# Gate columns of a hybrid layer's input projection: from weights stationary to activations stationary, with the heads' steps moved

## The reference

```python
h = rmsnorm(x, g_mix_pre);  proj = h @ w_in
mq, mk, mv, mo, mi, mf, rq, rk, rv, rg = split(proj)
mq, mk = silu(causal_dwconv([mq, mk]))
hm = head_rmsnorm(mlstm_chunkwise(mq, mk, mv, mi, mf), g) * sigmoid(mo)
hr = head_rmsnorm(retention_chunkwise(rotary(rq), rotary(rk), rv), g) * silu(rg)
x = x + rmsnorm(concat(hm, hr) @ w_out, g_mix_post)
h = rmsnorm(x, g_ffn_pre)
x = x + rmsnorm((silu(h @ w_gate) * (h @ w_up)) @ w_down, g_ffn_post)
```

## Time and profile before

| | us |
|---|---|
| median of 3 runs (1235.53 to 1236.18) | 1235.66 |
| the profiled execution: its time | 1235.49 |
| its span, first to last instruction | 1233.5 |
| busy: TensorE matmul / weight load | 1219.8 / 1026.0 |
| busy: VectorE / ScalarE / GpSimd | 704.3 / 598.9 / 12.4 |

### The profile page before, as it was taken

One profiled execution on the slowest core, in us unless ns is written; L12 is line 12 of the kernel. 1 busy time (PEld: TensorE's weight loads), 2 busy tenths in 40 slices (PEclk: granted clock), 3 DMA queues, 4 the chain that ended last, 5 costly groups with the idle time before them and its releaser, 6 DMA issues.

```text
span 1233.5 us, 15772 instructions
## 1 busy us (share of the span) xinstructions
PE 1219.8 (99%) x5907; PEld 1026.0 (83%) x5907; DVE 704.3 (57%) x898; ACT 598.9 (49%) x781; POOL 12.4 (1%) x35
## 2 busy tenths in 40 slices
PE   8999999999999999999999999999999999999997
PEld 7888888888888888888888888888888888888886
DVE  6656767777676646754554455454455454444444
ACT  5454666574655644644444444444444444343442
POOL 1000100000000000000000000000000000000000
PEclk9999999999999999999999999999999999999999
DMA  8566798967887566455565656565555665555551
GB/s 313 188 157 159 148 214 173 142 181 164 204 178 177 205 204 206 140 200 188 187 189 186 196 178 203 177 197 189 185 188 186 203 208 203 193 184 203 192 183 69
DMA packets 136936, 229.48 MB, mean 186 GB/s; under 512 B 6080, under 2 KB 55488, under 8 KB 136384
## 3 DMA queue, kind: packets, MB, share of 16 engines
q1 hardware_dynamic: 136608, 226.84, 62.9%
q0 software_dynamic: 288, 2.10, 0.5%
HBM read 226.83 MB, written 2.10 MB: 186 GB/s over the span
## 4 chain that ended last, share of the span: by engine, by line
PE 92%; DMA 4%; DVE 2%; ACT 1%; issue 0%; DVEq 0%; SPq 0%; ACTq 0%
PE bank L1142 91%; DMA raw<-in_w_in 3%; PE bank L1386 1%; DVE w_lo L726 1%; ACT w_hi L428 1%; DMA resid<-in_x 0%; DVE h L757 0%; PE bank L1304 0%; PE bank L1147 0%; DVE resid L1014 0%; ACT h L459 0%; PE bank L1359 0%; DVE gT L894 0%; ACT L555 0%; DVE pre L861 0%
## 5 line engine op out<-in xcount | busy, mean ns | idle before, releaser
L726 DVE TENSOR_TENSOR w_lo<-raw,w_hi 128x1024 fp32r<-128x1024 f32 x420 | 513.4, 1225 | 492.3 <-ACT w_hi L428 492.1
L428 ACT ACTIVATE w_hi<-raw 128x1024 fp32r<-128x1024 f32 x420 | 444.0, 1060 | 574.3 <-PE bank L1142 554.9
L1142 PE MATMUL bank<-w_hi,h2T 128*128 128x512 f32 x1376 | 426.6, 390 | 0.0
L1142 PEld LDWEIGHTS bank<-w_hi,h2T 128*128 128x128 f32 x1376 | 258.3, 188 | 53.4
L1142 PE MATMUL bank<-hT,w_hi 128*128 128x512 f32 x768 | 271.3, 397 | 0.0
L1142 PE MATMUL bank<-w_lo,h2T 128*128 128x512 f32 x688 | 267.7, 389 | 0.0
L1142 PE MATMUL bank<-w_hi,ffT 128*128 128x512 f32 x704 | 217.0, 389 | 0.0
L1142 PE MATMUL bank<-hT,w_lo 128*128 128x256 f32 x768 | 214.4, 279 | 0.0
L1142 PEld LDWEIGHTS bank<-hT,w_hi 128*128 128x128 f32 x768 | 144.0, 188 | 32.4
L1142 PEld LDWEIGHTS bank<-w_hi,ffT 128*128 128x128 f32 x704 | 132.2, 188 | 27.4
L1142 PEld LDWEIGHTS bank<-w_lo,h2T 128*128 128x128 f32 x688 | 129.2, 188 | 26.4
(11 more groups left out here) (159 smaller groups left out, 549.0 us busy)
## 6 DMA issues: line engine op xcount, KB each, us to landing
raw<-in_w_in SPq DMA_DIRECT2D x63, 1024.0 KB, 12.5
raw<-in_w_gate SPq DMA_DIRECT2D x44, 1024.0 KB, 5.2
raw<-in_w_up SPq DMA_DIRECT2D x44, 1024.0 KB, 5.1
raw<-in_w_down SPq DMA_DIRECT2D x44, 1024.0 KB, 5.0
raw<-in_w_out SPq DMA_DIRECT2D x16, 1024.0 KB, 5.1
resid<-in_x SPq DMA_DIRECT2D x2, 1024.0 KB, 5.9
out<-resid SPq DMA_DIRECT2D x8, 256.0 KB, 2.5
raw<-in_w_in SPq DMA_DIRECT2D x2, 512.0 KB, 8.5
```

The source lines that it names most:

```text
L428: act.activation(w_hi[:, s % AHEAD, :], raw[:, s // 2, (s % 2) * SUB:(s % 2 + 1) * SUB], ACT.Copy).then_inc(hi_done, 1)
L726: dve.tensor_tensor(w_lo[:, s % AHEAD, :], raw[:, s // 2, (s % 2) * SUB:(s % 2 + 1) * SUB], w_hi[:, s % AHEAD, :].bitcast(F32), ALU.subtra ...
L1142: return pe.matmul(out_, lhsT, rhs, start=start, stop=stop, skip_group_check=True)
```

## The change

The gate rounds use `sub_tokens` instead of `sub_columns`: one accumulator pair for a whole round, tokens on partitions. Their weights are loaded as 4 rows x 512 columns per partition instead of 8 x 256. ScalarE takes the sigmoid (or, for retention, silu) straight from the accumulators into `gate_out` at s = 7, `head_scaled` multiplies `y` by it, and `mix`, the gate sums, the gate's `copy_right` and the later multiplication by the pre-activation disappear. `mix_hi` and `mix_rest` now both read bank `B_T`. With the gate known only at the round's end, every head step starts four subs later (`HEAD_LAG`); `mix_hi` moves from 7 to 6 and `mix_rest` from 8 to 7 after the start, and `turned` (now `head_turned`) waits for `mix_lo`. Output groups 0 and 1 are interleaved: six subs of 0, six of 1, two of 0, two of 1, then group 2. TensorE's loop over groups becomes straight code.

```diff
+HEAD_LAG = 4
+OUT_SUBS = [(0, k) for k in range(6)] + [(1, k) for k in range(6)] + [(0, 6), (0, 7), (1, 6), (1, 7)]\
+    + [(2, k) for k in range(8)]
+OUT_ENDS = {13: 0, 15: 1, 23: 2}
...
-        n, odd = divmod(8 * (rnd - gate_round(group)) + s - first, 2)
+        n, odd = divmod(8 * (rnd - gate_round(group)) + s - HEAD_LAG - first, 2)
...
+                            if n == 2:
+                                src = in_rows(4 * q, 4, col, 512)
+                            else:
+                                src = in_rows(8 * (q % 2), 8, col + (q // 2) * 256, 256)
...
-                a = head_at(rnd, s, 7)
+                a = head_at(rnd, s, 6)
                 if a is not None:
-                    act.wait_ge(mix_ready, a + 1)
-                    act.activation(mixT[:, a, 0:SEQ], gT[:, a % 4, :], ACT.Copy).then_inc(mix_hi, 1)
+                    act.wait_ge(yT_done, a + 1)
+                    act.activation(mixT[:, a, 0:SEQ], bank[:, B_T, 0:SEQ], ACT.Copy,
+                                   scale=coef[:, C_GHEAD + a:C_GHEAD + a + 1]).then_inc(mix_hi, 1)
...
+                if is_gate(rnd) and s == 7:
+                    event = event_of(rnd, 0)
+                    act.wait_ge(acc_free, event + 2)
+                    for t in range(TT):
+                        ins = act.activation(gate_out[:, t, :], acc(pair_used(event))[:, t, :],
+                                             ACT.Silu if rnd >= gate_round(2) else ACT.Sigmoid)
+                    ins.then_inc(acc_free, 1)
...
+                dve.wait_ge(acc_free, event_of(gate_round(a // 4), 0) + 3)
                 for t in range(TT):
-                    ins = dve.tensor_scalar(y[:, a % 2, t, :], pv_out(a)[:, t, 0:HD],
-                                            head_stat(a, H_SCALE)[:, t:t + 1], None, ALU.mult)
+                    ins = dve.scalar_tensor_tensor(y[:, a % 2, t, :], pv_out(a)[:, t, 0:HD],
+                                                   head_stat(a, H_SCALE)[:, t:t + 1],
+                                                   gate_out[:, t, a % 4 * HD:(a % 4 + 1) * HD],
+                                                   ALU.mult, ALU.mult)
                 ins.then_inc(y_ready, 1)
-
-            def mix(a):
...
             def mix_rest(a):
                 dve.wait_ge(mix_hi, a + 1)
-                dve.tensor_tensor(mixT[:, a, SEQ:2 * SEQ], gT[:, a % 4, :],
-                                  mixT[:, a, 0:SEQ].bitcast(F32), ALU.subtract).then_inc(mix_lo, 1)
+                dve.scalar_tensor_tensor(mixT[:, a, SEQ:2 * SEQ], bank[:, B_T, 0:SEQ],
+                                         coef[:, C_GHEAD + a:C_GHEAD + a + 1],
+                                         mixT[:, a, 0:SEQ].bitcast(F32),
+                                         ALU.mult, ALU.subtract).then_inc(mix_lo, 1)
...
-                for step, first in ((weigh, 0), (mix, 6), (head_scaled, 4), (head_variance, 3),
-                                    (head_recip, 2), (mix_rest, 8)):
+                for step, first in ((weigh, 0), (head_scaled, 4), (head_variance, 3), (head_recip, 2),
+                                    (mix_rest, 7)):
...
+            def head_turned(a):
+                pe.wait_ge(y_ready, a + 3)
+                if a:
+                    pe.wait_ge(mix_lo, a)
                 for t in range(TT):
-                    ins = pe.transpose(bank[:, B_T, t * P:(t + 1) * P], y[:, n % 2, t, :], ident)
+                    ins = pe.transpose(bank[:, B_T, t * P:(t + 1) * P], y[:, a % 2, t, :], ident)
                 ins.then_inc(yT_done, 1)
...
+                if is_gate(rnd):
+                    event = event_of(rnd, 0)
+                    pe.wait_ge(acc_free, event + 1)
+                    for s in range(8):
+                        heads_in_front(rnd, s)
+                        sub_tokens(8 * rnd + s + 1, s % AHEAD, hT, pair_used(event), 2 * s, KT - 1)
+                        heads_behind(rnd, s)
```

More of the change, by code:

```diff
@@ L353, in _ @@
                         for q in range(4):
[L354 to L359, removed]
+                            col = COL_RET * kind + 512 * half + part * DH
+                            if n == 2:
+                                src = in_rows(4 * q, 4, col, 512)
+                            else:
+                                src = in_rows(8 * (q % 2), 8, col + (q // 2) * 256, 256)
+                            load(6 * kind + 3 * half + (R_IN + n), q, src)
+            for m in range(16):
+                g, k = OUT_SUBS[2 * m] if m < 12 else (3, 2 * (m - 12))
+                load(R_OUT + m // 4, m % 4, rows(w_out, 2 * k, 4, 512 * g, 512))
             with sp.Fori(0, FF_GROUPS) as i:
@@ L548, in mixer_step @@
                 if ended:
[L549 to L556, removed]
+                    event = event_of(rnd, ended[2])
+                    copy_right(pair_used(event), event)
+                if is_gate(rnd) and s == 7:
[5 more added lines that the diff above has]
+                    ins.then_inc(acc_free, 1)
                 ended = unit_at(rnd, s, 2)
-                if ended and ended[1] < 2:
+                if ended:
                     group, part, u = ended
@@ L1164, in sub_columns, with unit_columns @@
                 ins.then_inc(sub_done, 1)
[L1166 removed]
+            def unit_columns(rnd, unit, act_T, before, after):
+                event = event_of(rnd, unit)
                 pe.wait_ge(acc_free, event + 1)
@@ L1305, in turned @@
                 ins.then_inc(yT_done, 1)
-            def gate_units(group, rnd, event):
-                def before(s):
-                    if s % 2 == 0:
-                        scores(group, s // 2)
-                def after(s):
-                    if s % 2 == 1:
-                        weighted(group, s // 2)
-                        if s >= 5:
-                            turned(group, (s - 5) // 2)
-                for u in range(2):
-                    unit_columns(rnd, u, event + u, hT, before, after)
@@ L1344, in _, with heads_in_front @@
[L1344 to L1351 removed]
+            def heads_in_front(rnd, s):
+                a = head_at(rnd, s, 0)
+                if a is not None:
+                    scores(a)
@@ new lines, in heads_behind @@
+            def heads_behind(rnd, s):
+                for step, first in ((weighted, 1), (head_turned, 5)):
+                    a = head_at(rnd, s, first)
+                    if a is not None:
+                        step(a)
+                if (rnd, s) == (R_IN, 3):
+                    pe.wait_ge(gates_act, 1)
+                    pe.wait_ge(gates_dve, 2)
+                if (rnd, s) == (R_IN, 6):
+                    gate_columns()
+                if rnd == R_IN + 1 and s == 0:
+                    spread_rows()
```

143 lines of the change are left out of this document (59 added, 84 removed).

## The result

The changed kernel takes **1254.25 us** (median of 4 runs, 1252.89 to 1256.39) beside 1235.92 us of the kernel before on the same chip: ratio 1.0143, 95% interval 1.0129 to 1.0158. That is 18 us slower, four times the 4.3 us that were forecast, and outside the range. The profiled execution took 1252.89 us with a span of 1251.2 us, 17.7 us more than the 1233.5 us of before.

A forecast was written before the change was run, and what follows sets the result against it. TensorE's matmuls, 91% of the chain, were taken as the bound. Gains of 4.1 us against waits of 7.8 and 0.9 gave +4.6 us, about 1240.0 us for the median, 0.35% slower; range 1232.5 to 1242.5 us.

The forecast's parts named there:

- the line on loads: Gate weights arrive in 2 KB runs, not 1 KB; ScalarE sometimes waits for such loads, TensorE does not: costed at nothing.
- the one on straight code: TensorE runs at full pace both in the loop and outside it, so writing the loop out was costed at nothing.
- The wait that the change adds: TensorE's transposes wait until `mix_rest` frees bank `B_T`: 7.8 us behind sub 13 plus 0.9 behind sub 15.
- behind sub 13: Sixth sub of the next q round, counting from the gate round's start: waits of 2.7, 2.3, 2.3 and 0.5 us.
- Behind sub 15: Last sub of the next q round: `w_lo`, then `mix_rest`; 0.2 us in three groups, 0.36 in the output projection, sum 0.9.
- the bold rule: An unobstructed VectorE head step ends about one sub late, just when TensorE comes to its own step of the same number.
- Rivals A and B: A: waits absent or small, 1231.6 to 1233.8 us, 17%. B: half the waits, 1235.9 us, 18% with what falls short of 2.5.
- The gain of 4.1 us: TensorE's total saving: 1.6 us from the gate rounds' form, 2.2 from the excess, 0.3 from a wait in the output projection.
- The term of 2.2 us for the excess: Extra 1.35 and 0.87 us in the 13-sub stretches of groups 0 and 2 should go through the head steps' four-sub lag.
- its 0.4 us per gate round: Gate subs by tokens take 2.72 us instead of 2.77: 0.05 us each, 1.6 us over 32 subs.
- Rival C: Matmul pace set half by weight load, half by columns: token form gains 11 us, 1229 even with all waits; 3%.
- Rival D: The gate activation's cover is gone too, at `head_scaled`: up to 1 us more in four groups, 1244 us; 12%.

The follow-up runs named there:

- e1: The kernel before with only TensorE's loop over the three groups written out as straight code; 1252.10 us, ratio 1.0116.
- e3: The changed kernel with q, k and gate weights all loaded as 4 rows of 512 columns (2 KB runs); 1243.44 us, ratio 1.0051.
- e15: The kernel of e2 with one more input of 1.5 MB that no instruction reads; 1235.90 us, ratio 0.9992.
- e2: The changed kernel with `mix_rest` issued a step earlier and first in VectorE's turn; 1249.73 us, ratio 1.0098.
- e10: The kernel of e2 with all these weight loads in 2 KB runs, as in e3; 1233.91 us, ratio 0.9987.
- e9: The kernel before with all loads of the projection's 12 rounds in 2 KB runs; 1235.01 us, ratio 0.9992.
- e13: The kernel before with one more input of 1 MB that no instruction reads; 1238.54 us, ratio 1.0029.
- e5: The kernel before with TensorE's loop over the feed-forward groups written out, nothing changed in the mixer; 1258.50 us, ratio 1.0182.
- e8: The kernel of e2 with one more input of 1 MB that no instruction reads; 1248.64 us.

## Why the prediction was wrong, by its steps

- **The step that failed is the line on loads, "ScalarE waits for such loads at times, TensorE does not, so no gain", with the one on straight code, "both at full pace": both were costed at nothing.** The heading promised their cover, and for the loads none was worked out. Loads landed up to 23.3 us after their issue in the kernel before, ScalarE waited for them 19.4 us in all, and at about 25 us TensorE waits on `w_lo`: a cover of 2 us at best. In one place there was none. The load of 23.3 us, issued at 134 us, landed at 157.4; ScalarE had waited for it, VectorE came late to `probs`, and TensorE waited for that, in the kernel before:

```profile
157.60 2.01 ACT L428 ACTIVATE w_hi<-raw 128x1024 fp32r<-128x1024 f32 x2 [2.23 <-DMA raw<-in_w_in]
```

```profile
163.83 0.93 PE L1142 MATMUL bank<-v_sb,probs 128*128 x6 [0.91 <-DVE probs L912]
```

  The edit that writes TensorE's code out was priced by its pace alone. In this kernel it changes how long loads take, and costs 1252.10 - 1236.85 = 15.3 us by itself in e1 (its own runs of before beside it). In the changed kernel the late loads are 1254.25 - 1243.44 = 10.8 us (e3; 11.7 us against each one's runs of before), or 13.8 us once the other wait is out of the way (e15 against e2).
- **The wait that the change adds was right in place, order and nearly in size.** The prediction had 2.7, 2.3, 2.3 and 0.5 us behind sub 13. Behind the q round of group 1, TensorE's last matmul starts at 210.27 and is done 0.11 later (half of one pace), the transpose starts at 213.13: 2.75 us. The other gaps are 2.35, 2.34 and some 0.4. VectorE's rows there are the ones that were counted, rotation or convolution first, `mix_rest` (line 973) after it, and the restart 0.15 us behind its end at 212.98:

```profile
211.64 0.87 DVE L910 SCALAR_TENSOR_TENSOR pre<-pre,columns,spin 128x256 f32<-128x256 f32 x2
212.43 0.16 DVE L953 TENSOR_SCALAR stat<-stat 128x2 f32<-128x2 f32 x1
212.50 0.48 DVE L973 SCALAR_TENSOR_TENSOR mixT<-bank,columns,mixT 128x256 fp32r<-128x256 f32 x1
```

  Behind sub 15 the gaps are 0.3, 0.2, 0.2 and 0.3 us, 1.1 in place of 0.9, so all gaps are 8.9 us where the term was 8.7. The 9.4 us between the spans of e3 and e10 hold these 8.9 us, 1.7 us of lower clock behind the first gap of e3 ((0.39 + 0.18) x 3, from 204 to 210 us; in the changed kernel the clock stayed at 1.00 behind the same gap) and 0.4 us of pace (below), less 1.7 us of gaps that e10 has itself: 9.3 us. Taking `mix_rest` one step earlier removes the wait, as the bold rule says, at the price of one of these: 1.3 us once in front of a transpose that waits for `y`, since VectorE now waits 1.9 us for ScalarE's half of `mixT`. Rivals A and B are out.
- **The gain of 4.1 us was too high.** The 13-sub stretches hold 41.79, 41.65 and 42.39 us (the differences in the table's rows) in place of 43.15, 41.80 and 42.67, 1.8 us less in three groups. In e3 against e9 the change costs 8.4 us with a wait of 9.5: a net gain of 1.1 us at most. The term of 2.2 us for the excess had a wrong cause: in e9, where only the loads differ from before and the heads' steps stand as they did, the stretches are 41.8, 42.0 and 41.9 us, and in e13 group 1 has the long one (43.7 us) and not group 0. The excess was late loads too, as the rows at 157.60 and 163.83 above show for group 0. And the form did not give its 0.4 us per gate round: from the start of group 1's gate round to the end of the q round behind it the kernel before takes 50.1 us and e10 50.7, where 49.7 was forecast. Of this 1.0 us the pace, the point below, is 0.4, and a gap of 0.2 is left in front of the transpose behind sub 13; the rest was not settled.
- **"Both at full pace" for straight code was wrong by a small amount.** Column subs run at two paces. e10, TensorE at the first matmul of two subs in an early round, and at the same matmul (the eighth) of two subs in a late one:

```profile
145.06 0.40 PE L1157 MATMUL bank<-hT,w_hi 128*128 128x512 f32 x1
...
147.88 0.40 PE L1157 MATMUL bank<-hT,w_hi 128*128 128x512 f32 x1
...
358.93 0.28 PE L1157 MATMUL bank<-hT,w_lo 128*128 128x256 f32 x1
...
361.70 0.28 PE L1157 MATMUL bank<-hT,w_lo 128*128 128x256 f32 x1
```

  2.82 us against 2.77. Counted over the sub starts of the trace, 5 column subs went at 2.82 to 2.83 us in the kernel before and 10 in e9, but 20 in e10 and 27 in e3: 17 more between e9 and e3 at 0.055 us, 0.9 us. What sets the pace was not settled: e13, the kernel before with an unread input, has 25.
- **Rival C is out**: the gate rounds by tokens gave no 11 us, not even without waits (e10), nor the 8 us that I had estimated beside it from the Trainium skill (TensorE: Matmul & The Clock Gate, Back-to-back issue gap); by that page's paces the measurement disagrees, with 227 ns for a matmul of 512 columns. **Rival D is out too**: the waits of the changed kernel have no line for a late gate activation of the size it needed, and the emptying of output group 0 stayed covered.
- The chance of "slower" (0.62) was right in sign, but the range had no case in which the loads become the bound. The prediction's range went to 1242.5; e3, where only the known terms act, is at 1243.44, 6.6 us over its own runs of before, which is 1242.3 from the prediction's 1235.66: just inside. (By the prediction's own list "same" is 0.18 and "faster" 0.20, where it says 0.19 for both.)

What stays open is the property of the memory behind it. These runs show that the length of a program and an unread input move it, that it goes where all these loads have 2 KB runs (which also read the rows in another order, so that the run length alone is not isolated), and that in e2's kernel 64 KB, 512 KB and 2 MB do nothing, 1 MB swaps the halves, and 1.5 MB brings back the landings of the kernel before. How the length of a program does it is open too: e5 brought 0.66 MB of instructions where before brings 0.43 MB, a smaller difference than the 512 KB that did nothing. The Trainium skill (DMA: Bandwidth & Descriptors, Latency and other measured facts) tells of copies that slow down when the rows of neighbouring partitions lie large powers of two apart, and gives aliasing of memory channels as an inference. `w_in` has 16 rows of 8208 floats for each partition, 513 KB apart, near such a distance; but the same row of the page has hardly any loss at 512 KB (207 GB/s, beside 214 for a padded one), for 16 KB per partition, where 1 KB runs moved 120 GB/s here. No run here varied the distance, so this is a pointer and not a finding.

## What to carry to other kernels

Before an edit that changes the length of a program or the set of its tensors is costed at nothing, read the landing times of the loads one by one, minimum to maximum, and how much later they may come until the bound engine waits; a cover of 2 us under a spread of 11 (12.5 to 23.3) is none. Follow each wait of the engine in front for a load down to the bound engine, under whatever name the last wait goes: here it was `probs`, and `floor` in the changed kernel. When a kernel with unchanged early code differs early, shift the placement alone (an input that nothing reads) before blaming an instruction. And where an engine's step moves behind a step of the same number on another engine, take it one step earlier: here that was worth 8.6 to 9.5 us once loads were not late, and 5.5 us while they were.

## What the runs showed of the hardware that was not expected

- Loads of 1 MB in runs of 1 KB landed after 6.9 to 32.5 us (both in e8), and the same loads at the same times differed by placement alone (e2 against e8), while with all these loads in runs of 2 KB they took 5.5 to 12.7 us (e3, e9, e10).
- Writing out a loop that runs after 480 us cost 22.6 us (e5, 1258.50 against 1235.91), all of it through loads of the mixer as far as its waits show. The Trainium skill (Runtime: NRT & Kernel Launch, Instruction fetch mechanics) says that kernels prefer full unrolling where they can; both loops written out here (e1, e5) made the kernel before slower, through its loads; with the placement of e15, a kernel with the first loop written out lost nothing.
- The DMA engines' busy share does not tell what they move: 0.93 at 122 GB/s and 0.75 at 195 GB/s.
- An idle of TensorE of 2.0 us was followed by a granted clock of 0.68 and 0.64 over 10 us, 3.4 us more. But one idle does not decide it: the clock stayed at 1.00 behind the 2.75 us gap at 210 us of the changed kernel, and in e9 it fell at 137 us behind sixteen matmuls on 8 rows with no idle that the waits show, for 1.7 us.
- Column subs of the same 16 matmuls take 2.77 or 2.82 us, and keep to the one or the other for rounds on end (e10: the slower one from group 0's k round to group 2's, the faster one in group 3's).
